# Attention stage of a hybrid encoder block: new places in the queues for its loads, and v and the gates loaded from Pool

## The reference

```
proj = h @ w_in           # fox q,k,v,f,z | swa q,k,v,z | merge gates
logits_fox = q.k/sqrt(64) + F[t] - F[s], causal; 8 heads of 64, softmax, @ v
logits_swa = q.k/sqrt(64) - slope*|dist|, window of 2 chunks of 64, a sink per head; 8 heads on 2 kv heads
ya = (fox * silu(z_a)) @ w_o_fox ;  yb = (swa * silu(z_b)) @ w_o_swa
x + gate * ((sigmoid(g_a)*ya + sigmoid(g_b)*yb) @ w_out)
```

## Time and profile before

| | |
|---|---|
| median of the runs | 2253.3 us |
| the profiled execution, its span | 2240.93 us, 2239.2 us |
| PE busy, granted clock | 91%, 0.929 |
| DVE, ACT, POOL busy | 41%, 34%, 25% |
| POOL: 382 subtractions L1008 | 420.0 us busy, 324.2 us idle before them |

### The profile page before, as it was taken

The page is one execution under the profiler, slowest core; times in us unless marked ns, Lnnn a source line. Parts: engine busy times, 40 slices in busy tenths (PEclk is TensorE's granted clock), DMA queues, the critical chain, the costliest instruction groups (busy, mean ns, idle before and its releaser), DMA issues. The chain is left out here.

```text
span 2239.2 us, 28292 instructions
## 1 busy us (share of the span) xinstructions
PE 2043.7 (91%) x9722; PEld 1632.9 (73%) x9722; DVE 922.6 (41%) x1916; ACT 755.2 (34%) x1439; POOL 557.2 (25%) x534
## 2 busy tenths in 40 slices
PE   7399999999999999999589889899898887998998
PEld 3277878887888788888456666566666667998887
DVE  2845565643121300000254455445544545564332
ACT  2522222210121421211147557566576662001100
POOL 1600000000000000000036547466475562120000
PEclk9599999999999999999779889788898988999999
DMA  6234343454221221211444342543535305242222
GB/s 236 85 106 122 94 122 90 140 151 109 94 85 47 83 84 48 84 66 52 138 90 103 79 117 69 122 105 74 117 90 112 80 23 193 76 131 94 94 94 85
DMA packets 230121, 222.98 MB, mean 100 GB/s; under 512 B 53682, under 2 KB 187698, under 8 KB 227444
## 3 DMA queue, kind: packets, MB, share of 16 engines
q1 hardware_dynamic: 218244, 181.74, 29.1%
q0 software_dynamic: 11648, 39.85, 5.6%
q10 hardware_dynamic: 128, 0.13, 0.0%
HBM read 149.58 MB, written 72.09 MB: 99 GB/s over the span
## 5 line engine op out<-in xcount | busy, mean ns | idle before, releaser
L1008 POOL TENSOR_TENSOR Pl<-PT,Ph 128x512 fp32r<-128x512 f32 (+2 forms) x382 | 420.0, 1116 | 324.2 <-ACT Ph L1138 254.5
L454 PE MATMUL pj<-hTh,Wh 128*128 128x512 f32 x768 | 299.4, 390 | 0.7 <-DVE Wl L646 0.4
L455 PE MATMUL pj<-hTl,Wh 128*128 128x512 f32 x768 | 298.8, 389 | 0.0
L456 PE MATMUL pj<-hTh,Wl 128*128 128x512 f32 x768 | 298.8, 389 | 0.0
L1131 ACT ACTIVATE PT<-sc 128x512 f32<-128x512 f32 (+2 forms) x382 | 199.0, 521 | 206.6 <-PE sc L1061 84.8
L454 PE MATMUL pj<-Wh,hTh 128*128 128x512 f32 (+1 forms) x640 | 245.3, 383 | 22.2 <-DVE Wl L646 22.2
L365 POOL DMA_DIRECT2D wraw<-in_w_in x84 | 45.1, 537 | 852.9 <-DVE Wl L646 847.2
L456 PE MATMUL pj<-Wh,hTl 128*128 128x512 f32 (+1 forms) x640 | 238.9, 373 | 0.0
L455 PE MATMUL pj<-Wl,hTh 128*128 128x512 f32 (+1 forms) x640 | 238.7, 373 | 0.0
L1138 ACT ACTIVATE Ph<-PT 128x512 fp32r<-128x512 f32 (+2 forms) x382 | 214.3, 561 | 12.1
L1216 DVE TENSOR_REDUCE part_max<-mx 128x1 f32<-128x512 f32 (+3 forms) x288 | 169.4, 598 | 90.8 <-PE mx L1033 89.2
(11 more groups left out here) (213 smaller groups left out, 3615.7 us busy)
## 6 DMA issues: line engine op xcount, KB each, us to landing
qk_scratch<-qThl SPq DMA_DIRECT2D x96, 256.0 KB, 2.8
wraw<-in_w_in POOLq DMA_DIRECT2D x88, 256.0 KB, 3.7
g_scratch<-st SPq DMA_DIRECT2D x64, 256.0 KB, 2.4
gt<-g_scratch SPq DMA_DIRECT2D x16, 1024.0 KB, 7.8
xin<-in_x POOLq DMA_DIRECT2D x16, 512.0 KB, 4.9
wada<-in_w_ada SPq DMA_DIRECT2D x8, 1024.0 KB, 7.5
z_scratch<-st SPq DMA_DIRECT2D x32, 256.0 KB, 2.4
Kb<-qk_scratch SPq DMA_DIRECT2D x8, 1024.0 KB
```

The source lines that it names most:

```text
L454: nc.tensor.matmul(out, a_hi, b_hi, start=first, stop=False)
L455: nc.tensor.matmul(out, a_hi, b_lo, start=False, stop=False)
L456: return nc.tensor.matmul(out, a_lo, b_hi, start=False, stop=last)
L1008: pool.tensor_tensor(Pl[n % NPH][0:rows, 0:w], PT[n % NP][0:rows, 0:w], Ph[n % NPH][0:rows, 0:w].bitcast(F32), ALU.subtract).then_inc(low_ ...
```

## The change

It computes the same. In `attend`:

- v and z are issued by Pool, between its subtractions: `load_v` two steps and `load_z` two steps later in step count than they stood on SP.
- On SP, q is placed AHEAD = 3 steps earlier; of k, `Ka` and the forget row likewise, then q, and only then `Kb` (`load_k_pairs`, with a semaphore of its own, waited for at the scores). Rows are stored and loaded at the head of a step; the load stands 5 steps after the row instead of 3.
- TILE_LEAD and ROW_LEAD grow by 2 steps.
- The sums' round trip has more room: `rs` loaded 5 steps after the batch (was 4), inverted at 9 (6), stored at 10 (7), `R` loaded at 13 (9), first scale at 18 (11). The last batches are 6 and 2 blocks instead of 4, 2 and 2; a batch starts no sooner than the one before has ended.
- At the start, the first loads are spread over the steps; DVE sets up only what the first tiles need, and the rest, with ACT's bias tables, after the first row.

```diff
-    TILE_LEAD, ROW_LEAD, SPACING = 14, 11, 0.8
+    TILE_LEAD, ROW_LEAD, SPACING = 16, 13, 0.8
...
-    k_due = when((h, START if h < 2 else last["f", (h - 2) * JB + 3] + 1) for h in range(FOX_H))
-    q_due = when((i, START if i < NQ else last["f", i - NQ] + 1) for i in range(NB))
-    v_due = when(((h, c), START if not h else last["f", h * JB - 1] - 15 + 4 * c + 4) for h in range(FOX_H) for c in range(JB))
-    s_due = when((t, START if t < 2 else last["s", 2 * t - 3] + 1) for t in range(TT))
-    z_due = when((e, START if e < NZ else last[blocks[e - NZ]] + 2) for e in range(NBLK))
+    k_due = when((h, START + 9 * h if h < 2 else last["f", (h - 2) * JB + 3] - AHEAD + 1) for h in range(FOX_H))
+    q_due = when((i, START + 2 * i if i < NQ else last["f", i - NQ] - AHEAD + 1) for i in range(NB))
+    v_due = when(((h, c), START + 3 + 2 * c if not h else last["f", h * JB - 1] - 15 + 4 * c + 6) for h in range(FOX_H) for c in range(JB))
+    s_due = when((t, START + 1 + 7 * t if t < 2 else last["s", 2 * t - 3] + 1) for t in range(TT))
+    z_due = when((e, START + 4 + 2 * e if e < NZ else last[blocks[e - NZ]] + 4) for e in range(NBLK))
...
-    for size in [8] * 7 + [4, 2, 2]:
+    for size in [8] * 7 + [6, 2]:
...
+        turns.append(max(last[blocks[e + size - 1]] + 5, free))
+        free = turns[-1] + 13 + size
+    sum_load = when(enumerate(turns))
+    invert_at = when((k, n + 4) for k, n in enumerate(turns))
+    inv_store = when((k, n + 5) for k, n in enumerate(turns))
+    inv_load = when((k, n + 8) for k, n in enumerate(turns))
+    scale_at = when(((k, e), n + 13 + m) for k, n in enumerate(turns) for m, e in enumerate(range(batches[k][0], sum(batches[k]))))
...
             for n in range(START, NS + TAIL):
+                for kind, i in row_load(n):
+                    load_rows(kind, i)
+                for kind, i in row_store(n):
+                    store_rows(kind, i)
                 for h in k_due(n):
                     load_k(h)
                 for i in q_due(n):
                     load_q(i)
-                for h, c in v_due(n):
-                    load_v(h, c)
+                for h in k_due(n):
+                    load_k_pairs(h)
                 for t in s_due(n):
                     load_s(t)
-                for e in z_due(n):
-                    load_z(e)
...
-            for n in range(NS):
+            for n in range(START, NS):
+                for h, c in v_due(n):
+                    load_v(h, c)
+                for e in z_due(n):
+                    load_z(e)
```

More of the change, by code:

```diff
@@ L835, in attend @@
-    TAIL = 14
+    turns, free = [], START
+    for e, size in batches:
+        turns.append(max(last[blocks[e + size - 1]] + 5, free))
[5 more added lines that the diff above has]
+    scale_at = when(((k, e), n + 13 + m) for k, n in enumerate(turns) for m, e in enumerate(range(batches[k][0], sum(batches[k]))))
@@ L837, in attend @@
+    TAIL = 22
     with ctx:
@@ L865, in attend @@
                 (PT[2][0:HD, 0:CHUNK], PT[2][0:HD, CHUNK:2 * CHUNK])]
-        k_in, s_in = ([sem(f"a_{n}{k}") for k in range(2)] for n in ("k", "s"))
+        k_in, kb_in, s_in = ([sem(f"a_{n}{k}") for k in range(2)] for n in ("k", "kb", "s"))
         q_in, z_in = [sem(f"a_q{k}") for k in range(NQ)], [sem(f"a_z{k}") for k in range(NZ)]
@@ L920, in load_s @@
                     sp.dma_start(VB[u][:, :, 0:P].bitcast(F32), dram["v"][t * P - CHUNK:t * P, FOX_H:, :]).then_inc(s_in[u], 16)
[L922 to L933, removed]
             def store_rows(kind, i):
@@ L1000, in _, with load_z, load_v @@
                 pool.memset(VB[k][:, :, P:3 * HD].bitcast(F32), 1.0).then_inc(ready, 1)
-            for n in range(NS):
+            def load_z(e):
+                kind, i = blocks[e]
+                if e >= NZ:
+                    pool.wait_ge(y_done, e - NZ + 1)
+                if kind == "f":
+                    source = dram["z"][i // JB * HD:(i // JB + 1) * HD, i % JB * QW:(i % JB + 1) * QW]
+                    tile = Z[e % NZ][0:HD, :]
+                else:
+                    t, g = i // 2, i % 2
+                    source = dram["z"][FW + g * GH * HD:FW + (g + 1) * GH * HD, t * P:(t + 1) * P].rearrange("(h d) n -> d h n", d=HD)
+                    tile = Z[e % NZ][0:HD, :].rearrange("d (h n) -> d h n", n=P)
+                pool.dma_start(tile, source).then_inc(z_in[e % NZ], 16)
+            def load_v(h, c):
+                if h:
+                    pool.wait_ge(pv_done, last["f", h * JB - 1] - 15 + 4 * c + 4)
+                rows = slice(c * QW, (c + 1) * QW)
+                pool.dma_start(V[:, c * JB:(c + 1) * JB, 0:P].bitcast(F32), dram["v"][rows, h, :].rearrange("(t p) n -> p t n", p=P)
+                             ).then_inc(v_in[c], 16)
+            for n in range(START, NS):
[3 more added lines that the diff above has]
+                    load_z(e)
+                if n < 0:
+                    continue
                 rows, w = shape_of(n)
@@ L1118, in _, with tables @@
             nc.scalar.activation(identr[:], ident[:], ACT.Copy).then_inc(bias_ready, 1)
[L1119 to L1122, removed]
+            def tables():
+                for k, bias in enumerate((biasM, biasA, biasB)):
+                    act.wait_ge(dist_ready, k + 1)
+                    for h in range(SWA_H):
+                        nc.scalar.activation(bias[:, h, :], dist[k][0], ACT.Copy, scale=-slope(h)).then_inc(bias_ready, 1)
             def exp(n):
@@ L1160, in _ @@
                         high_row(u)
+                        if (kind, i) == ("f", 0):
+                            tables()
                     elif kind == "s" and (a, c) == (KV_H - 1, 1):
@@ L1172, in _ @@
             st = Steps(dve, dve_steps)
[L1173 to L1176, removed]
+            nc.vector.memset(Ka[0][HD:HD + 4, :].bitcast(F32), 1.0).then_inc(cleared, 1)
             for k in range(NQ):
-                nc.vector.memset(Qa[k][HD:HD + 2, :].bitcast(F32), 1.0).then_inc(ready, 1)
```

69 lines of the change are left out of this document (36 added, 33 removed).

## The result

The median fell from 2251.6 to 2228.5 us (4 runs each): ratio 0.990, 95% interval 0.987 to 0.993. The profiled execution took 2225.7 us (span 2224.0) against 2240.9. A gain of 96 us was forecast; 23 us came in the medians and 15 in the profiled executions.

What follows compares the result with a forecast made beforehand. PE stops for q and behind DVE's waits for rs and R, with half clock after them, were taken to bound attention. Cycles 80 + last stretch 11 + opening 8 - tail 3 = 96 us, from 2253.3 to 2157 us, range 2128 to 2210.

Steps and rivals of the forecast that it cites:

- What bounds the kernel: Attention cycles: PE stops for q and at swa tiles behind DVE, plus half clock after them, lose 16.4 us per cycle.
- the 98 us: Time the six cycles of 91 us lose against the clean rate: 548 us taken, 449.7 at that rate.
- the clean rate: 0.221 us per matmul, read from the attention stretch 1160 to 1222 us at clock 1.00.
- q earlier, and ahead of Kb: SP loads in attention: net 5.7 us gained on a q wait of at most 3.5 us, so it goes.
- the q stop: PE's wait for q once per head, 14.2 us in 6 waits, laid to bytes queued on SP.
- rs and R: Sums' round trip: DVE's waits mostly go, perhaps 1 us left at the scale; PE's stops at swa tiles go.
- behind the scale no tiles stand now, only the other scales, so PE does not notice: DVE's order after R: a remaining wait of perhaps 1 us at the scale costs PE nothing.
- What is late next: Swa rows behind k, q and Kb: new 1.2 us stop per cycle; 3 us taken, leaving 80 us gained.
- half remains: Rival: a stop of 2 us or more per cycle stays, costing 8 us per cycle; 2193 us, chance 0.24.
- v and z on Pool: 96 load issues at 0.6 us each on Pool, covered by its idle time: 0 on the path, 58 us uncovered.
- Opening: Start of attention: fewer bytes ahead of the first tiles bring the first score 6 to 12 us sooner; 8 taken.
- Last stretch and tail: End of attention: 11 of 16.4 us regained in the last stretch; later rs of the last blocks costs 3 us.

Runs made afterwards that it cites:

- e3_both: Changed kernel with swa rows loaded two steps earlier and scales three steps apart in the first six batches; 2178.7 us, 0.972 of the kernel before.
- e10_no_scale: e3_both with the scaling multiplications left out, so without the division by the sums; 2144.5 us in one run.
- e7_batches_alone: Kernel before with only the changed kernel's batch places (sum load, inversion, R, scales; sizes 6 and 2 at the end); 2208.8 us, 0.984 of before.
- e14_kq_alone: Kernel before with only k and q loaded three steps earlier and Kb behind q; 2234.0 us, 0.992 of before.
- e6_vz_alone: Kernel before with only the loads of v and the gates issued by Pool, two steps later; 2237.2 us, 0.995 of before.
- e1_rows: Changed kernel with the swa rows loaded two steps earlier, ahead of k, q and Kb; 2194.0 us, 0.980 of the kernel before.
- e4_vz_sp: Changed kernel with the loads of v and the gates back on SP at the same steps; 2245.5 us, 1.000 of the kernel before.
- e8_q1: e3_both with the second block's Q loaded right behind the first's, ahead of Kb and first swa loads; 2178.8 us, 0.971 of the kernel before.
- e13_ahead_of_kb: e2_spread with the swa rows one step earlier, behind k and q but ahead of Kb; 2188.6 us, 0.971 of the kernel before.
- e5_one_in: e3_both with the scales multiplying by constant 1 instead of R, leaving out the division by the sums; 2162.2 us, 0.961 of the kernel before.
- e2_spread: Changed kernel with the eight scales three steps apart in the first six batches; 2218.1 us, 0.989 of the kernel before.

## Why the prediction was wrong, step by step

- *What bounds the kernel*: right as to the stops and to the clock behind them. e3_both took 0.237 us per matmul at clock 0.99 in its profiled execution, so most of the 98 us could be had. But the clean rate was read ahead of the first batch, in a stretch without a scale. With scales and no long stops the cycle is 80.1 us, without them 76.9; the 75 us that the rate gives were nearly reached only without scales (75.8, the last four cycles of e10_no_scale).
- *q earlier, and ahead of Kb*: the q stop went, as forecast. k was issued at 1210.66, 1.3 us later than the 1209.4 of the prediction.
- *rs and R*: DVE's waits fell from 30 and 61 us to 5.3 and 5.0, as forecast:

```profile
DVE rs L1280 <- DMA rs<-sums: 5.3, 2, 3.7
DVE yT L1287 <- DMA R<-inv: 5.0, 1, 5.0
```

  **The step "behind the scale no tiles stand now, only the other scales, so PE does not notice" failed.** It priced the scales at nothing, with rows of 0.68 us at hand; twelve took 15.7 us, the collect behind them was late, and PE stopped 1.16 and 1.94 us. In before the first scales ran while Pool stood still, in the stop behind R, and the others fell mostly into gaps of 0.9 to 3.2 us between its subtractions:

```profile
1246.37 0.86 DVE L1268 TENSOR_TENSOR yT<-yT,R 64x256 f32<-64x256 f32 x2
1249.73 0.72 POOL L1008 TENSOR_TENSOR Pl<-PT,Ph 64x256 fp32r<-64x256 f32 x1 [6.96 <-PE ot L1104]
```

  Where DVE's wait for R is gone the scales of 64x256 take 1.1 to 1.4 us in every run (1425 ns in e7_batches_alone). Where some of it is left they took 496 ns (e14_kq_alone, 15.4 us of wait) and 801 (e6_vz_alone, 25.7). So the removal of the stop removed their cover; no run removes it and leaves the scales in their old places. The earlier trace rows shows a scale and a subtraction at one time, and was read for what the scale does to Pool and not for what Pool does to DVE. Undone with the rows already in place (e1_rows to e3_both) this is worth 0.8%. The profiles give 3.7 us per cycle for it, but 2.9 of them come from the one cycle of 95.6 us.
- *What is late next*: the right wait, mis-sized. **1.2 us (0 to 3) was put for it, 3 us per cycle with the clock; measured 3.7 us (3.0 to 4.4 but for one of 2.5), and 6.1 us per cycle with the clock (e1_rows, one profile each).** The bytes ahead were counted from 1209.4 as if the rows left with k; they left at 1213.26, behind five issues, and landed 10.1 us after that. This case stood among the rivals ("half remains", 2 us or more at the swa rows *or* behind R, 8 us per cycle) but as one stop; both came, 11.9 us per cycle above the 78 forecast.
- *v and z on Pool*: right. The issues took 61.9 us (0.58 and 0.77 us each), 58 were taken; PE's waits for Pl are tenths (0.4 at most). Back on SP it costs 1.0% (e4_vz_sp), with gates that come late; alone, moving them is worth 0.5% (e6_vz_alone).
- *Opening*: 8 taken, 2.4 measured (first score 1137.40), or 3.8 if it is counted from the last store of the stage ahead, which was issued 1.4 us later than in before. The first tile came at 1106.97, 5.3 us sooner, but the second block's q (Q1) stood behind the swa loads and ended its wait at 1121.08, not by 1116. e8_q1 shows that DVE's set-up is the next limit there, so little more was to be had.
- *Last stretch and tail*: the stretch took 61 us for 255 matmuls, 11 us less than at before's rate, and 11 were forecast. The tail cost 3.4 us (PE idle ahead of the merge 21.70 against 18.32), 3 forecast.

```profile
1846.73 0.55 PE L1389 MATMUL pa<-yh,woh 128*128 128x256 f32 x1 [21.70 <-DVE wol L1326]
```

In the sum: the cycles were to give 80 us, 13.3 each; the changed kernel got 1.6 each, e3_both in its profile 11.4. By the ratios, the two failed steps are 1.8 of the 3.3 points that were missing (0.957 forecast, 0.990 measured). The opening is 0.2, and the scales' own time (3 us per cycle, an estimate from the one run of e10_no_scale) some 0.8. That leaves some 0.5 without a run of its own; e3_both's lower clock in most executions would fit. Not settled: why the clock falls behind some gaps of about 1 us (e1_rows, e3_both, e13_ahead_of_kb) and not behind others, and where e5_one_in's last per cent comes from.

## What to carry over

When a stop is taken away, ask what ran for free during it: that work comes back, at the price that it has beside busy engines. When a load moves ahead in a queue, every small load that it passes gets its bytes in front; find the reader of each and move the small ones first (16 KB behind 1 MB of Kb cost 1.7%, e2_spread against e13_ahead_of_kb). Test each part alone: here one part (e7_batches_alone, 1.6%) was worth more than all of them together (1.0%).

## What the runs showed of the hardware

A multiplication of 64x256 in SBUF alone took 0.43 us (two in 0.86) while Pool stood, 1.1 to 1.4 us in the mean beside Pool's subtractions, with two operands (1383 ns in e3_both) or with one (1086 ns in e5_one_in); reading PSUM it took 0.41 us in all of these runs.

The granted clock fell to its lower level (1.2 GHz) behind two gaps of 0.84 and 1.06 us 3.3 us apart (e13_ahead_of_kb). It also fell behind single gaps: one of 0.98 us (e1_rows, at 1473.19) and one of 1.35 us, shown here in PE's timeline of e3_both by matmuls of 512 columns that start 0.42 to 0.43 us apart, where they start 0.23 apart at 2.4 GHz:

```profile
1343.68 0.37 PE L1032 MATMUL mx<-ident,nmax 128*4 128x128 f32 x1 [1.35 <-DVE nmax L1245]
1344.28 0.63 PE L1076 MATMUL sc<-Qb,Kb 128*128 128x512 f32 x1
1344.70 0.63 PE L1116 MATMUL ot<-Ph,V 128*128 128x512 f32 x1
```

Other single gaps of 1.2 us, one or two per cycle, left it at 2.4 GHz. So in these runs the length of a gap alone does not tell whether the clock falls.
